# Two transformer blocks in fp32 on one core: eight experts behind branches, or in one pipeline with a late loop

## The chip, the cores and the metric

One Trainium2 chip, one core of it. The metric is the device time of one execution in microseconds, lower is better. The kernel before was timed three times. Its profile is of one further execution.

## The reference

The input is one sequence of 256 tokens with 1024 features, all fp32. A first block of two layers (feed-forward parts, an attention and recurrence mixer, a short convolution mixer) is followed by a second block of two layers. The last sub-layer of the second block is a mixture of experts, and it is where the change lies:

```python
logits = x @ w_router + b_router            # 256 tokens x 8 experts
top_vals, top_idx = top_k(logits, 2)        # softmax over the two gives the weights
y[token] = sum over its two experts e of weight * (silu(x @ w_gate[e]) * (x @ w_up[e])) @ w_down[e]
```

w_gate and w_up are 1024 x 3584 for each expert, w_down is 3584 x 1024. After it come a gate row, a scaled residual and a layer norm. With 256 tokens and two experts each there are 512 places, 64 for an expert on average.

## The kernel before

**Tiles.** Every weight matrix is read in units: unit n is 1 MB of gate and up columns (`w_gu[n]`, 128 hidden columns of each) and 0.5 MB of down rows (`w_d[n]`). The mixture has 8 x 28 = 224 units. SyncE issues the loads (`load_moe_gu` L338, `load_moe_d` L346) into four buffers each, and a load waits until VectorE is through with the unit that lay there, four units earlier. Each fp32 weight is split in two fp32r parts: ScalarE makes the high part (`moe_hi_gu` L622, `moe_hi_d` L629), VectorE the low part (`moe_lo_gu` L1285, `moe_lo_d` L1290). The split parts have two buffers each. A product is three matmuls, high by high, high by low, low by high (`mm3`, L1565 to L1567).

**A mixture step.** For unit i TensorE does gate and up (`slot_gate_up`, 24 matmuls over 256 columns), transposes the product h of unit i - 1 (L1964) and adds the down product of unit i - 2 (`slot_down`, 6 matmuls over 512 columns) to PA. ScalarE does silu (L654), the high part of h (L660), the high parts of units i + 2 (gate and up) and i (down). VectorE does the product with up (L1302), the low part of h (L1308), and the low parts of units i - 1 (down) and i + 2 (gate and up).

**Slots.** The tokens of an expert are gathered into 128 slots by a one-hot matmul (L1917). The outcome of an expert is copied from PA to YS by ScalarE (L689), multiplied by the transposed one-hots with the weights (`scatter_previous`, L1924) at steps 3 and 5 of the following expert, and added to ACC by VectorE (L1314). The next tokens are gathered at steps 16 and 17.

**Branches.** The router's result is counted per expert (`members`, s5i). Before the first expert ScalarE, VectorE and TensorE each load all eight counts into registers (L702, L1407, L2057). Each expert then stands in an If on its count: `sparse(e)` for up to 128 tokens (L1345, L671, L1976), `dense(e)` over all 256 tokens otherwise (L1376, L691, L2032). The bodies of all experts are written out one after the other, with short loops (`Fori`) inside. `sparse(e)` ends with its own pipeline empty: the last two down products and the copy to YS are inside it.

```python
                    with pe.If(counts[e] <= P):
                        sparse(e)
                    with pe.Else():
                        dense(e)
```

**In front of the mixture.** `pre(b)` transposes the normalized tokens (L1621), ScalarE and VectorE scale them into XTF (`modulated`, L449 and L845) and split XTF into XH and XL (`high` L460, `low` L852). TensorE waits for all of XL (L1896) and then computes the logits (L1899) from XTF. VectorE makes the residual (L869, L872), clears ACC (L1229), and does the routing in small operations (L1232 to L1262).

**Behind it.** TensorE scatters the last expert (L1924 into acc), VectorE applies the gate row and the layer norm (L905 to L919), ScalarE its squares and roots (L410, L393, L400), SyncE writes the two halves out.

Of the kernel before, what the change touches and what calls it, by code (L numbers as in the profile page):

```python
# [22 lines left out]
F32 = mybir.dt.float32  # L23
F32R = mybir.dt.float32r
I32 = mybir.dt.int32
ALU = mybir.AluOpType
# [3 lines left out]
P = 128  # L30
# [69 lines left out]
def program(nc, A, out):  # L100
    with ExitStack() as ctx:
# [48 lines left out]
        def view(at, n):  # L150
# [71 lines left out]
        members = s5i[0:1, 0:NE]  # L222
# [41 lines left out]
            "acc", "wT_sb", "hf", "hT", "hh", "gate", "base")}  # L264

# [103 lines left out]
        def _(act):  # L369
# [43 lines left out]
            def pre(b):  # L413
# [52 lines left out]
                for j in (0, 1):  # L466
                    modulated(j)
                high(0)
# [175 lines left out]
            def moe(b):  # L644
# [17 lines left out]
                def sparse_step(i, at, first=False):  # L662

                    silu(i, at, P)
                    if not first:
# [5 lines left out]
                def sparse(e):  # L671
                    at = e * NF2
                    sparse_step(0, at, first=True)
                    for i in range(1, 8):
                        sparse_step(i, at)
                    with act.Fori(0, 2) as j:
                        for i in range(8, 12):
                            sparse_step(i, at + j * 4)
                    for i in range(16, 20):
                        sparse_step(i, at)  # L680
                        if e + 1 < NE and i in (17, 18):
                            gathered(e + 1, i - 17)
                    for i in range(20, NF2):
                        sparse_step(i, at)
                    moe_hi_d(NF2 - 1, at)
                    h_hi(NF2 - 1, at)
                    moe_hi_gu(NF2 + 1, at)
                    act.wait_ge(d_used, at + N0 + NF2)
                    act.activation(YS, tile2(PA[:, 0:2, :]), ACT.Copy).then_inc(moe_s["y"], 1)  # L689

                def dense(e):  # L691
                    with act.Fori(0, NF2 // 4) as j:
                        for i in range(4):
                            at = e * NF2 + j * 4
                            silu(i, at, S)
                            moe_hi_gu(i + 2, at)
                            moe_hi_d(i, at)
                    if e + 1 < NE:
                        gathered(e + 1, 0)
                        gathered(e + 1, 1)  # L700
# [24 lines left out]
        def _(dve):  # L725
# [93 lines left out]
            def pre(b):  # L819
# [36 lines left out]
                if b > SECOND:  # L856
                    dve.wait_ge(xn_done, 2 * b)
                low(0)
# [360 lines left out]
            def moe(b):  # L1219
# [42 lines left out]
                dve.tensor_copy(s5i[:, 0:NE], PB[:, 2, 48:56]).then_inc(moe_s["routed"], 1)  # L1262
# [3 lines left out]
                def onehots(dst, e, weight):  # L1266
                    for t in range(NT):
                        where = place[:, t, e:e + 1]
                        if weight:
                            last = TS(dst[:, t], SLOT, where, share[:, t, e:e + 1], ALU.is_equal, ALU.mult)  # L1270
# [64 lines left out]
                def sparse_step(i, at, first=False, last=False):  # L1335

                    if not last:
                        gated(i, at, P)
                    if not first:
                        h_lo(i - 1, at, PA[:, 2 + (N0 + i - 1) % 2, 0:P], P)  # L1340
                        moe_lo_d(i - 1, at)
                    if not last and i < NF2 - 1:
                        moe_lo_gu(i + 2, at)

                def sparse(e):  # L1345
                    at = e * NF2
                    sparse_step(0, at, first=True)
                    for i in range(1, 9):
# [868 lines left out]
```

## Time and profile before

| | us |
|---|---|
| median of 3 runs | 3064.76 (3061.61 to 3068.96) |
| the profiled execution's own time | 3065.1 |
| span of its profile | 3063.3 |
| outside the span | 1.8 |
| PE, DVE, ACT, POOL busy, share of the span | 87%, 74%, 48%, 31% |
| mixture, first gate-and-up matmul to the last copy to YS | 1933.1 to 3044.3 |

Times in rows are microseconds from the start of the span. Engines are PE (TensorE matmuls), PEld (its weight loads), DVE (VectorE), ACT (ScalarE), POOL (GpSimd), SP (SyncE). A name with a q behind it is the engine's sequencer. The number in square brackets behind a row is the idle time of the engine just before, and what ended it; "issue" means that nothing in the profile was waited for. Matmuls overlap, so their durations are longer than the distance from one to the next. PEclk is the granted TensorE clock, 1.00 for 2.4 GHz and 0.50 for 1.2 GHz.

### The profile page before, as it was taken

How to read it: one execution, taken by the hardware profiler on the slowest of the kernel's cores; microseconds unless marked ns; L12 is line 12 of the kernel's file. 1: busy time of each engine (PE TensorE's matmuls, PEld its weight loads, DVE VectorE, ACT ScalarE, POOL GpSimd, SP SyncE). 2: the span in 40 equal slices, each digit the busy share in tenths (PEclk: the TensorE clock that was granted, in tenths of full speed). 3: DMA queues.
4: the chain of work that ended last, by engine and by line, in shares of the span. 5: the costliest groups of instructions: out<-in, count | busy, mean ns of one | idle time of the engine just before them, and what ended most of it. 6: DMA issues, size and time to landing. Idle time of an engine off the chain costs nothing.

```text
span 3063.3 us, 46911 instructions
## 1 busy us (share of the span) xinstructions
PE 2679.0 (87%) x17674; PEld 2428.0 (79%) x17674; DVE 2255.6 (74%) x2506; ACT 1468.6 (48%) x1892; POOL 953.6 (31%) x568
## 2 busy tenths in 40 slices
PE   8997699999988995569996556899999999999998
PEld 7997589999977984359995435788898989898887
DVE  6676467767768556957677695787787878787788
ACT  4343443433443342043333203676666767676666
POOL 6960079699128003308995330000000000000000
PEclk9998699999999996789997687899999999999999
DMA  7753167577444541137752113698898889798876
GB/s 293 259 192 131 62 228 253 213 253 252 150 161 157 185 156 61 35 110 267 256 199 85 61 35 117 252 341 301 298 343 308 327 299 338 300 343 296 331 278 238
DMA packets 129229, 670.87 MB, mean 219 GB/s; under 512 B 14672, under 2 KB 14992, under 8 KB 80064
## 3 DMA queue, kind: packets, MB, share of 16 engines
q1 hardware_dynamic: 111024, 604.72, 53.7%
q0 software_dynamic: 18064, 64.21, 6.1%
q8 instruction: 96, 1.57, 0.2%
q14 instruction: 45, 0.37, 0.0%
HBM read 667.82 MB, written 1.05 MB: 218 GB/s over the span
## 4 chain that ended last, share of the span: by engine, by line
PE 78%; DVE 14%; ACT 4%; issue 3%; POOL 1%; DMA 1%; ACTq 0%; SPq 0%; DVEq 0%
PE work L1565 16%; PE work L1566 15%; PE work L1567 15%; PE acc L1565 8%; PE acc L1567 8%; PE acc L1566 8%; DVE wl_gu L1285 1%; DVE scratch L1194 1%; ACT wh_gu L622 1%; PE work L1917 1%; PE work L1924 1%; PE acc L1964 1%; DVE wl_gu L735 1%; DVE rows L1133 1%; DVE xT_lo L832 1%
## 5 line engine op out<-in xcount | busy, mean ns | idle before, releaser
L1565 PE MATMUL work<-xT_hi,wh_gu 128*128 128x256 f32 x2120 | 610.7, 288 | 49.9 <-DVE xT_lo L852 19.5
L1566 PE MATMUL work<-xT_lo,wh_gu 128*128 128x256 f32 x2120 | 608.5, 287 | 0.0
L1567 PE MATMUL work<-xT_hi,wl_gu 128*128 128x256 f32 x2120 | 607.4, 287 | 0.0
L1565 PE MATMUL work<-wh_gu,mixT_hi 128*128 128x256 f32 x1792 | 522.7, 292 | 43.2 <-issue 27.8
L1566 PE MATMUL work<-wl_gu,mixT_hi 128*128 128x256 f32 x1792 | 513.2, 286 | 2.6 <-issue 2.6
L1567 PE MATMUL work<-wh_gu,mixT_lo 128*128 128x256 f32 x1792 | 512.5, 286 | 0.2 <-issue 0.2
L735 DVE TENSOR_TENSOR wl_gu<-raw_gu,wh_gu 128x2048 fp32r<-128x2048 f32 x158 | 390.5, 2471 | 124.5 <-ACT wh_gu L375 124.0
L1565 PEld LDWEIGHTS work<-xT_hi,wh_gu 128*128 128x128 f32 x2120 | 415.3, 196 | 60.3 <-issue 35.2
L1566 PEld LDWEIGHTS work<-xT_lo,wh_gu 128*128 128x128 f32 x2120 | 415.9, 196 | 4.8
L1567 PEld LDWEIGHTS work<-xT_hi,wl_gu 128*128 128x128 f32 x2120 | 415.2, 196 | 0.0
L1565 PEld LDWEIGHTS work<-wh_gu,mixT_hi 128*128 128x128 f32 x1792 | 348.9, 195 | 59.2 <-issue 37.6
L1565 PE MATMUL acc<-wh_d,h_hi 128*128 128x512 f32 x912 | 379.3, 416 | 10.2 <-DVE wl_d L1290 8.5
L740 DVE TENSOR_TENSOR wl_d<-raw_d,wh_d 128x1024 fp32r<-128x1024 f32 x157 | 244.7, 1559 | 169.5 <-ACT wh_d L382 169.5
L1566 PEld LDWEIGHTS work<-wl_gu,mixT_hi 128*128 128x128 f32 x1792 | 349.8, 195 | 13.5 <-issue 6.1
L1566 PE MATMUL acc<-wl_d,h_hi 128*128 128x512 f32 x912 | 359.9, 395 | 0.0
L1567 PE MATMUL acc<-wh_d,h_lo 128*128 128x512 f32 x912 | 359.7, 394 | 0.0
L375 ACT ACTIVATE wh_gu<-raw_gu 128x2048 fp32r<-128x2048 f32 x158 | 301.3, 1907 | 112.6 <-PE acc L1567 62.8
L1567 PEld LDWEIGHTS work<-wh_gu,mixT_lo 128*128 128x128 f32 x1792 | 349.1, 195 | 0.6 <-issue 0.5
L382 ACT ACTIVATE wh_d<-raw_d 128x1024 fp32r<-128x1024 f32 x157 | 166.4, 1060 | 294.8 <-PE acc L1567 287.1
L1498 POOL TENSOR_TENSOR scratch<-scratch 128x1024 f32<-128x1024 f32 x84 | 292.2, 3478 | 7.0
L1285 DVE TENSOR_TENSOR wl_gu<-raw_gu,wh_gu 128x2048 fp32r<-128x2048 f32 x113 | 259.1, 2293 | 36.9 <-ACT wh_gu L622 36.7
L1285 DVE TENSOR_TENSOR wl_gu<-scratch,wh_gu 128x2048 fp32r<-128x2048 f32 x112 | 256.6, 2291 | 38.2 <-ACT wh_gu L622 37.9
(436 smaller groups left out, 4899.0 us busy)
## 6 DMA issues: line engine op xcount, KB each, us to landing
raw_gu<-in_w_gu SPq DMA_DIRECT2D x271, 1024.0 KB, 4.9
raw_d<-in_w_d SPq DMA_DIRECT2D x269, 512.0 KB, 5.1
scratch<-in_w_gu SPq DMA_DIRECT2D x112, 1024.0 KB, 7.0
scratch<-in_w_d SPq DMA_DIRECT2D x112, 512.0 KB, 7.7
scratch<-in_w_mod POOLq DMA_DIRECT2D x96, 512.0 KB, 3.7
scratch<-in_s_b POOLq DMA_DIRECT2D x16, 256.0 KB, 3.0
rows<-in_norm_post POOLq DMA_DIRECT2D x6, 512.0 KB, 4.3
rows<-in_ln_g POOLq DMA_DIRECT2D x4, 512.0 KB, 4.4
```

Source lines behind the costliest of these rows:

```text
L375: act.activation(wh_gu[k][:, :, :, :].rearrange("p a k n -> p (a k n)"), raw_gu[k][:, :], ACT.Copy).then_inc(gu_hi, 1)
L382: act.activation(wh_d[k][:, :], raw_d[k][:, :], ACT.Copy).then_inc(d_hi, 1)
L622: act.activation(wh_gu[n % 2][:, :, :, :].rearrange("p a k n -> p (a k n)"), RAW_GU[k] if k > 1 else RAW_GU[k][:, :], ACT.Copy).then_inc(g ...
L735: TT(wl, raw_gu[k][:, :], wh.bitcast(F32), ALU.subtract).then_inc(gu_lo, 1)
L740: TT(wl_d[k][:, :], raw_d[k][:, :], wh_d[k][:, :].bitcast(F32), ALU.subtract).then_inc(d_lo, 1)
L832: last = STT(XL[:, k, tok], turned(t, k), C("norm_pre", 8 * b + k), XH[:, k, tok].bitcast(F32), ALU.mult, ALU.subtract)
L1133: TT(SC[:, 0:2], SC[:, 0:2], MT.rearrange("p (w h i) -> p w h i", w=2, h=4), ALU.add).then_inc(g["masked"], 1)
L1285: TT(wl, RAW_GU[k] if k > 1 else RAW_GU[k][:, :], wh.bitcast(F32), ALU.subtract).then_inc(gu_lo, 1)
L1498: TT(acc, acc, MW[n % 3], ALU.add).then_inc(mod_term, 1)
L1565: pe.matmul(out_, w[0], m[0], start=start, stop=False)
L1566: pe.matmul(out_, w[0], m[1], start=False, stop=False)
L1567: return pe.matmul(out_, w[1], m[0], start=False, stop=stop)
```

## The change

The eight Ifs and all of `dense` go. The steps of all experts form one pipeline: step 0 of an expert also does the transpose of the previous expert's unit 27 and the down product of its unit 26, and step 1 the down product of its unit 27. ScalarE's copy to YS moves into step 1 of the next expert. Only the last expert drains. The one-hots of an expert are made by VectorE just ahead of its step 0. ScalarE and VectorE each have one more loop over steps 20 to 27. In the last expert, ScalarE and VectorE now do the high and low part of the unit behind the last one (`moe_hi_gu(29)`, `moe_lo_gu(29)`) inside step 27, ahead of the last down unit. The counts are replaced by the largest of them (`most_members`), one register load for each engine behind the last expert, and an If around a loop for tokens beyond 128 slots. In `pre`, the split of XTF is left out for the mixture, and TensorE waits for XTF alone.

```diff
+        most_members = s5i[0:1, NE:NE + 1]
         # pre(b), ScalarE (VectorE has modulated(3), modulated(5))
+                if b == len(SUBS) - 1:
+                    modulated(2)
+                    modulated(4)
+                    return
         # ScalarE, moe
-                    if i < NF2 - 1:
-                        moe_hi_gu(i + 2, at)
-                        moe_hi_d(i, at)
+                    moe_hi_gu(i + 2, at)
+                    if i == 1 and e:
+                        act.wait_ge(d_used, N0 + at)
+                        act.activation(YS, tile2(PA[:, 0:2, :]), ACT.Copy).then_inc(moe_s["y"], 1)
+                    moe_hi_d(i, at)
...
-                counts = [act.value_load(members[:, e:e + 1], min_val=0, max_val=S) for e in range(NE)]
-                for e in range(NE):
-                    with act.If(counts[e] <= P):
-                        sparse(e)
-                    with act.Else():
-                        dense(e)
+                h_hi(NF2 - 1, (NE - 1) * NF2)
+                act.wait_ge(d_used, N0 + NE * NF2)
+                act.activation(YS, tile2(PA[:, 0:2, :]), ACT.Copy).then_inc(moe_s["y"], 1)
+
+                most = act.value_load(most_members, min_val=0, max_val=S)
+                with act.If(most > P):
...
         # VectorE, moe
-                dve.tensor_copy(s5i[:, 0:NE], PB[:, 2, 48:56]).then_inc(moe_s["routed"], 1)
+                link(dve.reduce_max(w1[:, 0:1], PB[:, 2, 48:56], AX.X))
+                dve.tensor_copy(s5i[:, NE:NE + 1], w1[:, 0:1]).then_inc(moe_s["routed"], 1)
+                def step(i, at, e=0):
+
+                    gated(i, at, P)
+                    if i or e:
+                        h_lo(i - 1, at, PA[:, 2 + (N0 + i - 1) % 2, 0:P], P)
+                        moe_lo_d(i - 1, at)
+                    moe_lo_gu(i + 2, at)
+
+                for e in range(NE):
+                    at = e * NF2
+                    last = onehots(WGT, e, True)
+                    if e + 1 < NE:
+                        last = onehots(ONE, e + 1, False)
+                    last.then_inc(moe_s["onehots"], 1)
+                    for i in range(8):
+                        step(i, at, e)
...
+                at = (NE - 1) * NF2
+                h_lo(NF2 - 1, at, PA[:, 2 + (N0 + NF2 - 1) % 2, 0:P], P)
+                moe_lo_d(NF2 - 1, at)
+
+                most = dve.value_load(most_members, min_val=0, max_val=S)
+                with dve.If(most > P):
...
         # TensorE, moe
-                pe.wait_ge(xt_l, 4 * (b + 1))
+                pe.wait_ge(xt_f, 4 * (b - SECOND + 1))
+                pe.wait_ge(xt_raw, 2 * (b - SECOND + 1))
...
+                    pe.wait_ge(moe_s["xg_l"], 2 * e + 2)
                     slot_gate_up(0, at, xg)
+                    if e:
+                        h_transpose(-1, at)
+                        slot_down(-2, at, False, False)
                     slot_gate_up(1, at, xg)
                     h_transpose(0, at)
+                    if e:
+                        slot_down(-1, at, False, True)
                     slot_gate_up(2, at, xg)
                     h_transpose(1, at)
                     if e:
                         pe.wait_ge(moe_s["y"], e)
                     slot_down(0, at, True, False)
...
+                h_transpose(NF2 - 1, at)
+                slot_down(NF2 - 2, at, False, False)
+                slot_down(NF2 - 1, at, False, True)
+
+                most = pe.value_load(most_members, min_val=0, max_val=S)
+                with pe.If(most > P):
+                    pe.wait_ge(moe_s["y"], NE)
+                    with pe.Fori(0, NE) as e:
...
```

The lines beginning with # in this diff are headings. The late body is, for each of the 8 experts, one gather (16 matmuls), two transposes, a loop over the 28 units with its own loads on ScalarE's queue and single buffers (24 matmuls, a transpose, 6 matmuls, each step waiting for the one before), and one scatter (4 matmuls).

## Rows read from the trace of the kernel before

**Rows 1.** Page, the chain that ended last, by engine.

```profile
PE 78%; DVE 14%; ACT 4%; issue 3%; POOL 1%; DMA 1%; ACTq 0%; SPq 0%; DVEq 0%
```

**Rows 2.** Busy by window: us, PE, PEld, DVE, ACT, POOL, PEclk, DMA share, GB/s.

```profile
2120.00:2150.00 30.00, 30.00 (x215) 28.14 (x214) 26.84 (x29) 21.78 (x29) 0.00 (x0) 1.00 0.97 360
...
2069.10:2073.90 4.80, 4.80 (x22) 4.80 (x23) 0.00 (x0) 0.00 (x0) 0.00 (x0) 0.50 0.62 254
2074.80:2077.70 2.90, 2.90 (x25) 2.90 (x26) 0.82 (x2) 2.64 (x3) 0.00 (x0) 1.00 0.02 6
```

**Rows 3.** Timeline, ACT silu: steps 2 and 27 of experts 0, 1, 7.

```profile
1946.44 0.28 ACT L654 ACTIVATE scratch<-work 128x128 f32<-128x128 f32 x1 [2.91 <-PE work L1567]
2059.42 0.28 ACT L654 ACTIVATE scratch<-work 128x128 f32<-128x128 f32 x1 [1.18 <-PE work L1567]
...
2082.69 0.28 ACT L654 ACTIVATE scratch<-work 128x128 f32<-128x128 f32 x1 [1.53 <-PE work L1567]
...
2199.10 0.28 ACT L654 ACTIVATE scratch<-work 128x128 f32<-128x128 f32 x1 [1.18 <-PE work L1567]
...
2920.12 0.28 ACT L654 ACTIVATE scratch<-work 128x128 f32<-128x128 f32 x1 [0.65 <-PE work L1567]
...
3038.27 0.28 ACT L654 ACTIVATE scratch<-work 128x128 f32<-128x128 f32 x1 [1.18 <-PE work L1567]
```

**Rows 4.** Waits, 1942 to 3041 us: total us, times, longest us.

```profile
PE work L1565 <- issue: 27.8, 7, 4.8
...
PE work L1565 <- DVE wl_gu L1285: 12.2, 8, 2.7
```

**Rows 5.** Branches of the experts on TensorE (2000:3043) and VectorE: ns min/median/max.

```profile
L2060 PEldq COMPARE_BRANCH  x15: 78/3807/6207, 2063.7 to 3042.6; - x15
...
L1413 DVEq COMPARE_BRANCH  x16: 43/47/54, 1937.6 to 3042.9; - x16
```

**Rows 6.** Timeline, one steady step of expert 1.

```profile
2123.56 2.29 DVE L1285 TENSOR_TENSOR wl_gu<-raw_gu,wh_gu 128x2048 fp32r<-128x2048 f32 x1 [0.35 <-ACT wh_gu L622]
...
2125.64 0.28 ACT L654 ACTIVATE scratch<-work 128x128 f32<-128x128 f32 x1 [1.17 <-PE work L1567]
...
2126.95 0.28 PE L1565 MATMUL work<-wh_gu,mixT_hi 128*128 128x256 f32 x1
```

**Rows 7.** Down weights: timeline of issue and use, then issue to landing.

```profile
2119.05 1.06 ACT L629 ACTIVATE wh_d<-raw_d 128x1024 fp32r<-128x1024 f32 x1
...
2122.18 0.51 SPq L346 DMA_DIRECT2D raw_d<-in_w_d  x1
...
2132.15 1.05 ACT L629 ACTIVATE wh_d<-raw_d 128x1024 fp32r<-128x1024 f32 x1
...
DMA to landing us min/median/max: 5.4/7.8/9.7
```

**Rows 8.** Timeline, in front of the mixture and its first steps.

```profile
1904.09 1.18 ACT L460 ACTIVATE xT_hi<-scratch 128x512 fp32r<-128x512 f32 x2
...
1906.32 0.79 ACT L449 ACTIVATE scratch<-acc,cols 128x128 f32<-128x128 f32 x2
...
1908.91 6.97 PE L1899 MATMUL work<-router_w,scratch 128*128 128x8 f32 x32 [5.48 <-DVE xT_lo L852]
...
1936.14 1.28 ACT L654 ACT_TABLE_LOAD   x1 [3.96 <-issue]
...
1937.46 0.61 DVE L1270 TENSOR_SCALAR scratch<-scratch,small 128x128 f32<-128x128 f32 x2 [4.56 <-issue]
...
1941.89 0.58 PE L1565 MATMUL work<-wh_gu,mixT_hi 128*128 128x256 f32 x1 [2.69 <-DVE wl_gu L1285]
```

**Rows 9.** Timeline, the end of the last expert.

```profile
3042.88 2.29 DVE L1285 TENSOR_TENSOR wl_gu<-raw_gu,wh_gu 128x2048 fp32r<-128x2048 f32 x1 [0.38 <-ACT wh_gu L622]
...
3044.26 1.02 ACT L689 ACTIVATE scratch<-acc 128x1024 f32<-128x1024 f32 x1 [1.41 <-PE acc L1567]
...
3046.55 5.37 PE L1924 MATMUL acc<-scratch 128*128 128x512 f32 x8 [2.32 <-issue]
```

More of the change, by code:

```diff
@@ L264, in program @@
             "acc", "wT_sb", "hf", "hT", "hh", "gate", "base")}
+        late = {n: sem("late_" + n) for n in ("gu_landed", "d_landed", "sum", "scattered", "added")}
+        U1, H1 = N0 + NE * NF2, M0 + NE * NF2
         T_OF = {"ab": 16, "mix2": 9}
@@ L702, in moe @@
[L702 to L707 removed]
+                    with act.Fori(0, 2) as j:
+                        for i in range(20, 24):
+                            step(i, at + j * 4)
+                h_hi(NF2 - 1, (NE - 1) * NF2)
+                act.wait_ge(d_used, N0 + NE * NF2)
@@ L1407, in moe @@
-                counts = [dve.value_load(members[:, e:e + 1], min_val=0, max_val=S) for e in range(NE)]
-                for e in range(NE):
-                    last = onehots(WGT, e, True)
-                    if e + 1 < NE:
-                        last = onehots(ONE, e + 1, False)
-                    last.then_inc(moe_s["onehots"], 1)
-                    with dve.If(counts[e] <= P):
-                        sparse(e)
-                    with dve.Else():
-                        dense(e)
+                            for i in range(8, 12):
+                                step(i, at + j * 4)
@@ new lines, in moe @@
+                        for i in range(16, 20):
+                            step(i, at)
+                            if i in (18, 19):
+                                xg_lo(e + 1, i - 18)
+                        with dve.Fori(0, 2) as j:
+                            for i in range(20, 24):
+                                step(i, at + j * 4)
+                        continue
+                    for i in range(8, NF2):
+                        step(i, at)
+                        if i == 11:
+                            gate_row()
+                        if i in (13, 15, 17, 19):
+                            base((i - 13) // 4, (i - 13) // 2 % 2)
@@ L1974, in slot_down, with step @@
                     last.then_inc(d_used, 1)
-                def sparse(e):
+                pe.wait_ge(moe_s["onehots"], 1)
+                gather(0)
+                gather(1)
+                for e in range(NE):
                     at, xg = e * NF2, e % 2
-                    def step(i, at):
+                    def step(i, at, xg=xg):
                         slot_gate_up(i, at, xg)
@@ L2054, in moe @@
-                pe.wait_ge(moe_s["onehots"], 1)
-                gather(0)
-                gather(1)
-                counts = [pe.value_load(members[:, e:e + 1], min_val=0, max_val=S) for e in range(NE)]
-                for e in range(NE):
-                    pe.wait_ge(moe_s["xg_l"], 2 * e + 2)
-                    with pe.If(counts[e] <= P):
-                        sparse(e)
-                    with pe.Else():
-                        dense(e)
+                h_transpose(NF2 - 1, at)
+                slot_down(NF2 - 2, at, False, False)
```

241 lines of the change are left out of this document (113 added, 128 removed).

## The prediction

> **What bounds the kernel now.** I read the chain of waits on the page first: TensorE carries 78% of it [rows 1]. Then the windows inside the mixture: in 30 us in the middle of an expert TensorE is busy for all 30, at the full clock of 1.00 (2.4 GHz), VectorE for 26.8 and ScalarE for 21.8; the transfers run at 360 GB/s with a share of 0.97 [rows 2]. So a steady step is bound by TensorE, with the transfers close behind. Its length is 4.37 us: the down split on ScalarE starts at 2119.05 and, three steps later, at 2132.15, so 13.10 / 3 [rows 7].
>
> Then the seams between experts, from the times of silu on ScalarE, which follows TensorE's gate and up directly [rows 3]. From silu of step 2 to silu of step 27 take 112.98 us in expert 0, 116.41 in expert 1 and 118.15 in expert 7. Experts 2 to 6 also take 116.41 each. The extra over 25 steps (109.2) is scatter, transposes and gather on TensorE, in expert 7 a wait for the gate row, and all of that stays. From step 2 of expert 0 to step 27 of expert 7 there are 3038.27 - 1946.44 = 1091.8 us; take away 112.98 + 6 x 116.41 + 118.15 = 929.6 and 162.2 us are left for seven seams, 23.2 each. A seam holds three steps, 13.1 us. So a seam loses 10.1 us.
>
> The waits say of what: 27.8 us in seven pieces of "issue", and 12.2 us for the low part of gate and up, of which 2.7 lie in front of the first expert's step 2 and the rest at the seams [rows 4]. The issue time is TensorE's sequencer in its branch at L2060, which takes 3.8 us in the median and up to 6.2, while the branch of VectorE at L1413 takes 0.05 [rows 5]. Behind that idle time TensorE restarts at clock 0.50 (1.2 GHz): 22 matmuls in 4.80 us, 0.218 each, against 25 in 2.90 us, 0.116 each, some microseconds later [rows 2]. 27.8 + 9.5 us are 5.3 us for a seam; the low clock on the 24 to 25 matmuls of step 0 is some 2.5; what is left of the 10.1 is the drain, where the last two down products wait for their splits one after the other.
>
> **The change part by part.** The sum is made against the profiled execution: 3065.1 us, of which the span is 3063.3 and 1.8 lie around it. The median of the runs is 3064.76, so the two are the same for this purpose.
>
> *Seams.* In the new order the matmuls of a seam are the same, and each wait becomes that of a steady step: down product of unit 26 in step 0, of unit 27 in step 1. So a seam costs three plain steps: -7 x 10.08 = -70.5 us. What could be late in its place:
> (a) The copy to YS, 1.02 us [rows 9], now stands on ScalarE in step 1 between two splits. ScalarE idles 1.17 us in each step before silu [rows 6], so it fits, barely. TensorE needs YS free only at the down product of step 2, and behind the copy the down split of unit 1 comes 1 us later, which VectorE takes up only in step 2. Cost 0; without that idle time, up to 1.0 for each seam.
> (b) The one-hots on VectorE, two operations of two instructions, 0.61 us for the first pair [rows 8] and as a bound the same for the second, now stand ahead of step 0. VectorE waits 0.35 us in each step for the high part [rows 6]. Its low part then ends at 2123.56 + 2.29 = 2125.85, and TensorE takes it at 2126.95, so there is another 1.1 us of cover [rows 6]. 1.2 us at most against 1.45: cost 0, at worst 1.2 for each seam.
> (c) The transfers lose the seam's rest. Behind SyncE's issue of a down load at 2122.18 ScalarE uses that slot's unit at 2132.15, 10.0 us later; landing takes 7.8 us in the median, 9.7 at most [rows 7]. A load that lands later than that is covered by ScalarE's 1.17 us. A full expert will take 116.4 + 13.1 = 129.5 us for 28 x 1.573 MB = 44.0 MB, 340 GB/s, under the 360 that the steady window already moves [rows 2]. Cost 0; as an upper bound 1 us for each expert.
>
> The Trainium skill, "DMA: Bandwidth & Descriptors" (Specifications), speaks against this change: it gives some 358 GB/s of HBM for a core. By it a steady step would be bound by memory and take an estimated 1.573 MB / 358 = 4.39 us in place of 4.37, some +5 us over 8 x 25 such steps. This trace is already a little over it, with 360 GB/s at a share of 0.97 [rows 2]; the mechanism is rival 2.
>
> *In front of the mixture.* The logits start at 1908.91. Of their input the last piece on ScalarE is made from 1906.32 to 1907.11, behind three copies into XH of which two take 1.18 us together [rows 8] and the third, of half the width, by an estimate from that row 0.3. Without them the input is complete at about 1905.7, -3.0 us with the waits around it (bounds: -1.8, if ScalarE's piece stays at 1907.1; -6.4, if the logits, 6.97 us for 32 records or 0.218 each, also ran at the full clock's 0.116 [rows 2, 8]). VectorE's residual and clearing of ACC start as much earlier and stay beside the logits. The added maximum over the counts is one small operation in VectorE's chain, +0.2 us.
>
> *First expert.* ScalarE stands 3.96 us and VectorE 4.56 us in "issue", their eight register loads; ScalarE then loads its table for 1.28 us before silu of step 0 [rows 8]. Without the register loads the table load falls in the wait for the first gate and up, and silu, both splits and step 2 of TensorE come 1.3 us earlier: its wait of 2.69 us [rows 8] becomes 1.4. Step 2 also ran at the low clock: silu came 1946.44 - 1941.89 = 4.55 us after its start [rows 3, 8], where 24 matmuls at 0.12 take 2.9. At the seams a wait of some 1.4 us (9.5 / 7, [rows 4]) follows 25 matmuls at the full clock; I take it that the shorter wait here keeps the clock too: -1.65. Together -3.0; bounds -1.0 and -4.5.
>
> *End.* In step 27 of the last expert the split of the unit behind the end is now ahead of the last down split. VectorE's low part of it, 2.29 us, stood behind before, at 3042.88 [rows 9]; in front, it starts when ScalarE has the high part, some 0.6 us after VectorE would have begun with unit 27. I take +1.65 us for the last down product. Before, the scatter then waited for the branch until 3046.55, though the copy to YS was done at 3044.26 + 1.02 = 3045.28 [rows 9], 1.25 us earlier. Now one register load (3.96 / 8 = 0.5 us) and one branch over the late body stand there. Branches over short bodies are those of VectorE, 0.05 us; over the long dense body of TensorE, 3.8 [rows 5]. The late body on TensorE has some 60 matmuls where `dense` has about 280, so I take it as short: the copy sets the start, +1.65 - 1.25 = +0.4. As an upper bound it costs the full 3.8 again: +1.65 + 0.5 = +2.2.
> The Trainium skill, "Runtime: NRT & Kernel Launch" (Instruction fetch mechanics), says that a taken branch whose target isn't in the current two pages has to fetch it first; by it, too, the short body is the cheap case, and the long ones are what the change removes. No row shows the page size.
>
> Sum: -70.5 - 3.0 + 0.2 - 3.0 + 0.4 = -75.9, and 3065.1 - 75.9 = 2989.2. The span would be 2987.4.
>
> **The rivals.**
> 1. *The seam keeps a wait.* (a) and (b) are late together, 1.0 + 1.2 us for each of seven seams, with what (c) adds up to 2989 + 4 to 2989 + 22, so 2993 to 3011, middle 3000. For it: the cover is only 1.17 and 1.45 us for 1.02 and 1.2. Against: the costs fall in different steps on different engines, and a late step is made up in those that follow. Chance 0.13.
> 2. *The transfers fall behind over a full expert*, because the 360 GB/s of 30 us can't be held without the seam's rest. Landing then moves from its median towards its maximum and beyond, by 9.7 - 7.8 = 1.9 us [rows 7], of which ScalarE's idle time hides 1.17 [rows 6]: 0.7 us for each of eight experts, +6, so 2995. The page's rule on the HBM is of this kind. Against: 340 GB/s are wanted on average. Chance 0.08.
> 3. *Only the branch goes.* TensorE still starts an expert with the wait for its low part and the drain's waits, because a split of the next expert is late; only the 27.8 us of issue, the low clock (2.5 us for each seam) and the 6 us in front go: 3065.1 - 27.8 - 17.5 - 6 = 3014. For it: the drain's waits look like VectorE's. Against: in the new order no unit's split depends on the drain. Chance 0.05.
> 4. *The transfers become the bound.* If the average over an expert before (44.0 MB in 116.4 + 23.2 = 139.6 us, 315 GB/s) were what memory gives over a long stretch, the mixture would stay as long as it is, and only the 6 us in front would come: 3059. Against: 360 GB/s over 30 us [rows 2]. Chance 0.03.
> 5. *Slower: the late body is run.* It decides at 129 tokens in the busiest expert, where one If opens the loop for all eight experts. A unit there waits in series for its load (5.4 us at the least [rows 7]), a low part of 2.29 [rows 6], some 2.9 us of gate and up and, as an estimate from these, 2 for a high part and 1 for down: 13 us for 224 units, +2900 us, about 5900. Against: every one of the 8 experts took the slot form before, as its 28 silus of 128 columns show [rows 3]. Chance 0.01.
> 6. *It doesn't do what it says*, because the loops' exits on TensorE, now at the end of each expert, cost what the If cost: nothing gained at the seams, 3060. Against: such exits stand in the middle of the 116.41 us already, without a trace in them. Chance 0.02.
>
> **How the numbers follow.** The forecast itself, 2981 to 2995, has 0.68. The predicted time is that of its middle, 2989. The range takes in its bounds (-3.4 for a full clock under the logits and -1.5 in the first expert below, +1.8 at the end and +2.0 in the first expert above) rival 2 and half of rival 1: 2981 to 3004. A measurement of this kernel tells 0.2%, 6 us, from no change. Faster by more than that: 0.68 + 0.13 + 0.08 + 0.05 = 0.94, and 0.02 of rivals 4 and 6, which lie at the edge: 0.96. Within: 0.03. Slower: 0.01.
>
> **What would show it.** Right: silu to silu across a seam in three steps of 4.37 us, TensorE without "issue" waits in the mixture, granted clock 1.00 from the first expert's step 2 to the last drain, an expert in 129.5 us, no landing that ScalarE waits for, logits 3 us earlier, and the last unit's low part behind that of the unit after it. Wrong: waits of TensorE for a low part in steps 0 to 3, ScalarE's down split waiting for a load, a long branch in front of the last scatter, or any instruction of the late body.

## The result and the profile after

The kernel after takes 2988.94 us (median of four, 2986.70 to 2992.49), beside 3066.86 for the kernel before on the same chip: ratio 0.9747, 95% interval 0.9728 to 0.9767. A second set of five executions, run as the last experiment, gave 2991.48 and 0.9771 (0.9754 to 0.9788). The forecast was 2989.0, 2981 to 3004. The profiled execution took 2992.49 us with a span of 2990.7. One of the six executions of the last version below (both ends put right) ran in a slower state, 3441 us at a granted clock of 0.72, and is left out of its figures.

The chain that ended last, by engine (before: [rows 1]), and two windows, the second over a seam (columns as in [rows 2]):

```profile
PE 80%; DVE 13%; ACT 3%; issue 2%; POOL 1%; DMA 1%; SPq 0%; DVEq 0%; ACTq 0%
```

```profile
2120.00:2150.00 30.00, 30.00 (x222) 28.41 (x221) 23.69 (x25) 21.63 (x31) 0.00 (x0) 1.00 0.94 354
2060.00:2070.00 10.00, 10.00 (x72) 9.34 (x71) 9.63 (x16) 8.03 (x12) 0.00 (x0) 1.00 0.97 373
```

A seam is now full on TensorE at the full clock, as the middle of an expert is. All waits of TensorE from 1942 to 2970 us (before: [rows 4], 27.8 of issue and 12.2 for the low part of gate and up):

```profile
PE work L1647 <- DVE scratch L1343: 3.3, 1, 3.3
PE acc L1580 <- DVE wl_d L1315: 0.4, 1, 0.4
```

The timeline of the first seam, silu of step 27, VectorE's one-hots and its low part behind step 0, the copy to YS, silu of step 2 (before: [rows 3]):

```profile
2056.18 0.28 ACT L661 ACTIVATE scratch<-work 128x128 f32<-128x128 f32 x1 [1.17 <-PE work L1582]
...
2060.67 0.60 DVE L1295 TENSOR_SCALAR scratch<-scratch,small 128x128 f32<-128x128 f32 x2
2061.18 0.48 DVE L1297 TENSOR_SCALAR scratch<-scratch,small 128x128 f32<-128x128 f32 x2
...
2063.10 2.29 DVE L1310 TENSOR_TENSOR wl_gu<-scratch,wh_gu 128x2048 fp32r<-128x2048 f32 x1
...
2067.05 1.02 ACT L677 ACTIVATE scratch<-acc 128x1024 f32<-128x1024 f32 x1
...
2069.28 0.28 ACT L661 ACTIVATE scratch<-work 128x128 f32<-128x128 f32 x1 [0.25 <-PE work L1582]
```

2069.28 - 2056.18 = 13.10 us, and all seven seams take that. Before they took 162.24 together, now 91.70: -70.5. The low part of gate and up starts at 2063.10. The one before it started at 2058.46, and one plain step later would be 2058.46 + 4.37 = 2062.83, so it is 0.27 us late. ScalarE's idle time before silu fell from 1.17 to 0.25. TensorE waits for neither.

In front of the mixture and at its end (before: [rows 8, 9]): logits, first scatter; VectorE's last low parts, TensorE's last down products with their waits.

```profile
1907.82 6.24 PE L1915 MATMUL work<-router_w,scratch 128*128 128x8 f32 x32 [2.40 <-ACT scratch L452]
...
2968.27 2.29 DVE L1310 TENSOR_TENSOR wl_gu<-raw_gu,wh_gu 128x2048 fp32r<-128x2048 f32 x1 [0.35 <-ACT wh_gu L629]
...
2970.68 1.22 DVE L1315 TENSOR_TENSOR wl_d<-scratch,wh_d 128x1024 fp32r<-128x1024 f32 x1
...
2971.95 0.50 PE L1580 MATMUL acc<-wh_d,h_hi 128*128 128x512 f32 x1 [2.32 <-DVE wl_d L1315]
...
2974.73 3.70 PE L1940 MATMUL acc<-scratch 128*128 128x512 f32 x8 [1.11 <-ACT scratch L696]
```

Between landmarks of the two profiled executions (times at which the same instruction starts or ends in both) the 72.6 us between the spans are: seams -70.5; from the end of the second normalization to silu of the first expert's step 2, -5.3 (45.1 to 39.8); from the last silu to the end of the span, -0.3 (25.0 to 24.7); +1.5 inside the last expert (below); and +2.1 in code in front, which is the same in both. That last term is what one execution differs from the next by: the last operation of that normalization starts between 1895.8 and 1902.6 us in the fourteen profiles of before, after and the runs below, and in the two profiles of the kernel after it starts 2.9 us apart (1902.6 and 1899.7).

### The profile page after: what moved, and what is told of

The parts are those of the page before. It is cut to its first block, busy times and chain, and to the rows that moved or that the text cites. A ratio compares the mean times of both kernels' runs of the same rounds, so it can differ in the third digit from the quotient of the medians.

```text
span 2990.7 us, 47279 instructions
## 1 busy us (share of the span) xinstructions
PE 2657.8 (89%) x17674; PEld 2415.1 (81%) x17674; DVE 2255.8 (75%) x2501; ACT 1467.8 (49%) x1886; POOL 954.0 (32%) x568
## 3 DMA queue, kind: packets, MB, share of 16 engines
HBM read 667.82 MB, written 1.05 MB: 224 GB/s over the span
## 4 chain that ended last, share of the span: by engine, by line
PE 80%; DVE 13%; ACT 3%; issue 2%; POOL 1%; DMA 1%; SPq 0%; DVEq 0%; ACTq 0%
PE work L1580 16%; PE work L1581 16%; PE work L1582 16%; PE acc L1580 9%; PE acc L1582 9%; PE acc L1581 9%; DVE scratch L1217 1%; PE work L1933 1%; PE acc L1980 1%; PE work L1940 1%; DVE wl_gu L754 1%; DVE xT_lo L871 1%; DVE rows L1156 1%; DVE xT_lo L851 1%; PE work L1889 1%
## 5 line engine op out<-in xcount | busy, mean ns | idle before, releaser
L1580 PE MATMUL work<-wh_gu,mixT_hi 128*128 128x256 f32 x1792 | 514.3, 287 | 4.5 <-DVE mixT_lo L1303 3.3
L1581 PE MATMUL work<-wl_gu,mixT_hi 128*128 128x256 f32 x1792 | 506.9, 283 | 0.0
L1580 PEld LDWEIGHTS work<-wh_gu,mixT_hi 128*128 128x128 f32 x1792 | 342.3, 191 | 16.8 <-DVE mixT_lo L1303 3.5
L1581 PEld LDWEIGHTS work<-wl_gu,mixT_hi 128*128 128x128 f32 x1792 | 342.8, 191 | 11.6 <-issue 3.3
L1582 PEld LDWEIGHTS work<-wh_gu,mixT_lo 128*128 128x128 f32 x1792 | 342.6, 191 | 0.0
```

Of the source, the lines that this page charges most:

```text
L1580: pe.matmul(out_, w[0], m[0], start=start, stop=False)
L1581: pe.matmul(out_, w[0], m[1], start=False, stop=False)
L1582: return pe.matmul(out_, w[1], m[0], start=False, stop=stop)
```

## The experiments

Where a ratio is given, a run was timed four to six times beside the kernel before. The others are one execution each, with its profile; their totals settle nothing below some 6 us, and what they show is read from their traces.

**What the branch cost, and what the drain.** Two kernels, both the kernel before with its drained pipeline. In the first no expert has an If:

```diff
-    counts = [pe.value_load(members[:, e:e + 1], ...) for e in range(NE)]   # on all three engines
-    with pe.If(counts[e] <= P):
-        sparse(e)
-    with pe.Else():
-        dense(e)
+    sparse(e)
```

> The kernel before with the eight Ifs, the dense bodies and the register loads taken out; sparse(e) stays as it is, with its drain at each expert's end. Theory (a seam's 10.1 us are some 4.3 of branch, 2.5 of low clock behind it and 3.3 of drain and refill): no issue wait of TensorE at the seams, full clock there, a seam of 16.4 us from silu of step 27 to silu of step 2 in place of 23.2, and 3 us less in front of the first expert's step 2: about 3016 us. Rival A (the drain costs nothing by itself, the branch is all): seams of 13.1, about 2992. Rival B (the drain's waits alone are enough to lower the clock): seams of 19, about 3034.

In the second everything stays but most of TensorE's code that is never entered: of some 280 matmuls 14 are left, with the two scatters, which the expectation's 6 doesn't count (the part for more than 128 tokens is left out there).

```diff
     # TensorE, dense(e)
-    with pe.Fori(0, NF2 // 2 - 1) as j: ...
-    for i in (NF2 - 2, NF2 - 1): ...
-    next_tokens(e, 0)
-    next_tokens(e, 1)
```

> The kernel before with Ifs and register loads kept; only the body of dense(e) on TensorE, which is never entered here, is cut from some 280 matmuls to 6. Theory (what costs is how far the taken branch jumps): TensorE's branch at the end of sparse(e) takes under 0.5 us in place of 3.8 to 6.2, seams of 16.4 to 17 us, in all about 3018 us. Rival (an If's exit on TensorE costs this whatever it jumps over, because its queue of matmuls has to be refilled): seams of 23.2 as before, 3066 us.

Measured: 3014.89 us, ratio 0.9832 (0.9817 to 0.9846), and 3016.62, 0.9841 (0.9827 to 0.9855). A seam takes 16.5 us in both, in place of 23.2. The second kernel still has every If and register load; its branch, by the line that was L2060:

```profile
L2050 PEldq COMPARE_BRANCH  x16: 67/126/319, 1929.2 to 2992.4; - x16
```

and TensorE's waits in the mixture, the same in both kernels:

```profile
PE work L1565 <- DVE wl_gu L1285: 10.5, 7, 1.5
PE acc L1565 <- DVE wl_d L1290: 8.4, 16, 0.6
```

So 6.7 us of each seam hung on code of TensorE that is never run. Before, a seam had 4.4 us of issue time: the 27.8 us of [rows 4] and 2.8 more, of which 2.6 lie in the last seam, where TensorE stood still a second time, between two matmuls: 30.6 / 7. The other 2.3 are put down to the low clock behind it, which is a difference and not a row.

```profile
PE work L1566 <- issue: 2.6, 1, 2.6
```

The drain costs the other 3.4 (16.5 - 13.1). The wait for wl_gu, 1.5 us a seam, stands here without any issue time: it is the drain's, not the branch's. With 8.4 / 8 = 1.05 for wl_d these waits are 2.6 of the 3.4; no row names the rest.

The eight register loads are in the second kernel alone. From the first gate and up to silu of step 2 it takes 12.19 us, the first 10.81, but this isn't their price: both wait 1.50 us for wl_gu ahead of step 2, and the 1.4 us lie in step 0, which the second ran at a granted clock of 0.50 in its first 2 us, the first at 1.00. What they cost shows in the kernel before, which ran step 0 at 1.00 too: it waits 2.69 us in place of 1.50, and step 2, at the low clock behind that wait, takes 4.55 us to silu in place of 3.18. Together 2.6 us.

**Half of the code.** Between 280 matmuls (4.4 us of issue time) and 14 (nothing) lies a third length:

```diff
     # TensorE, dense(e) of the kernel before
-    with pe.Fori(0, NF2 // 2 - 1) as j: ...
```

> The kernel before, with the loop over 26 units taken out of the branch for more than 128 tokens on TensorE, which is not entered: the code that is jumped over shrinks from about 280 matmuls to about 160 for each expert; with nearly all of it gone (the run with a short else) the branch took 0.13 us and a seam 16.5. Theory (a far jump costs the same however far): branch of 3.8 us in the median, seam 23.2, total 3065. Rival 1 (the cost grows with what is jumped over): 57% of it, branch 2.2, seam about 20, total 3042. Rival 2 (it is short enough now): seam 16.5, total 3016.

Measured: 3045.80 us, and none of the three. The seven seams take 18.7, 16.5, 22.5, 22.9, 16.5, 23.5 and 24.0 us. The first matmuls behind the five that are not 16.5:

```profile
2067.18 0.28 PE L1565 MATMUL work<-wh_gu,mixT_hi 128*128 128x256 f32 x1 [2.08 <-issue]
...
2335.20 0.38 PE L1565 MATMUL work<-wh_gu,mixT_hi 128*128 128x256 f32 x1 [4.21 <-issue]
...
2474.12 0.37 PE L1566 MATMUL work<-wl_gu,mixT_hi 128*128 128x256 f32 x1 [4.15 <-issue]
...
2746.48 0.57 PE L1565 MATMUL work<-wh_gu,mixT_hi 128*128 128x256 f32 x1 [4.40 <-issue]
...
2887.21 0.57 PE L1565 MATMUL work<-wh_gu,mixT_hi 128*128 128x256 f32 x1 [5.23 <-issue]
```

The branches, and for comparison those of the kernel before:

```profile
L2055 PEldq COMPARE_BRANCH  x16: 67/186/6681, 1931.6 to 3025.3; - x16
```

```profile
L2060 PEldq COMPARE_BRANCH  x16: 78/1948/6207, 1932.9 to 3042.6; - x16
```

Half of the sixteen are the branches into an expert, under 0.1 us each in the kernel before. Of its eight jumps over the unentered body every one is long, 3.8 to 6.2 us. Here three of eight are (5.7, 5.9 and 6.7), and two stalls, of 2.08 and 4.15 us, stand behind jumps of 0.30 and 0.32 us; the second of them comes only after the first matmul of the step. So equal code over an equal distance costs nothing at two seams and at the end, and 2 to 5 us of idle time at five: the length alone doesn't decide. The copies differ in where they lie, and that this decides is the likely reading; no run moved a copy, and whether the same seams are hit in every execution wasn't looked at. The Trainium skill, "Runtime: NRT & Kernel Launch" (Instruction fetch mechanics), has a rule of this kind: a jump out of the two pages at hand waits for a fetch. Over equal code, branches of 5.7 to 6.7 us beside others of 0.3 agree with that; no run shows a page size or the fetch itself. The rows also show the clock: behind 2.08 us of idle time the matmuls go on at 0.28 us (granted clock 1.00 in the next 2.9 us), behind 4.15 us and more at 0.37 to 0.57 (granted clock 0.50 to 0.57).

**The split in front of the logits, put back** into the kernel after:

```diff
     # pre(b), ScalarE and VectorE
-                if b == len(SUBS) - 1:
-                    modulated(2)
-                    modulated(4)
-                    return
     # TensorE
-                pe.wait_ge(xt_f, 4 * (b - SECOND + 1))
-                pe.wait_ge(xt_raw, 2 * (b - SECOND + 1))
+                pe.wait_ge(xt_l, 4 * (b + 1))
```

> The changed kernel with the split of XTF and TensorE's wait for it put back in front of the logits. Theory: the logits start 3.0 to 3.2 us later behind the second normalization, 2992 us. Rival (VectorE's residual and the clearing of ACC bound this stretch anyway): less than 1 us, 2989 to 2990.

Measured: 2995.30 us, ratio 0.9773 (0.9759 to 0.9787), span 2993.2. The logits:

```profile
1909.41 6.96 PE L1906 MATMUL work<-router_w,scratch 128*128 128x8 f32 x32 [5.49 <-DVE xT_lo L867]
```

The wait is 5.49 us again, against 2.40 without the split: 3.1 us. In total the run doesn't settle so small a term; its interval overlaps with the second set of the kernel after. The landmarks do: from the end of the normalization to the start of the logits it is 7.6 us in all profiles with the split and 4.4 in all without it.

**How much cover the seam has on VectorE.** Expectation (b) of the forecast, loaded with more work:

```diff
     # VectorE, ahead of step 0
+    if e:
+        for m in range(4):
+            TS(view(3328 + P * m, P), SLOT, place[...], share[...], ALU.is_equal, ALU.mult)
+        TT(JUNK, X[:, 0, :], X[:, 1, :], ALU.mult)      # the second run alone
     last = onehots(WGT, e, True)
```

> The kernel after, with four more one-hot instructions (128 columns each) ahead of step 0 of experts 1 to 7. The four that are there take VectorE 0.90 us (2060.67 to 2061.57), so these add about as much. In the kernel after, the low part of gate and up in step 0 starts 0.27 us later than in a steady step, and TensorE takes it 1.10 us after its end. Theory (the cover is this 1.10 us): 0.27 + 0.90 = 1.17 late, so a seam from silu of step 27 to silu of step 2 takes 13.1 to 13.2 us, total within 1 us of the kernel after, 2989 us. Rival (each us on VectorE at a seam costs its us): seam 14.0, +6.3 us in all, 2995.

> As the run before, with one VectorE product of 1024 columns more (1.2 us), 2.1 us more than the kernel after at each seam. Theory (cover of 1.10 us, of which 0.27 are used): 0.27 + 2.1 - 1.10 = 1.3 us lost once at each seam, seam 14.4 us, a wait of TensorE for wl_gu in step 2, total 2989 + 9 = 2998; some more if the clock falls behind the wait. Rival (later steps take it up, nothing lost): 2989. Rival (all of it costs): seam 15.2, 3004.

Measured: 2995.91 and 3002.51 us; six seams of 13.48 and of 14.60, and a last one of 13.10 and 14.21. VectorE's low part of step 0 in the one and in the other:

```profile
2063.62 2.28 DVE L1310 TENSOR_TENSOR wl_gu<-scratch,wh_gu 128x2048 fp32r<-128x2048 f32 x1
```

```profile
2065.47 2.28 DVE L1310 TENSOR_TENSOR wl_gu<-scratch,wh_gu 128x2048 fp32r<-128x2048 f32 x1
```

By their own step 27 (2057.95 and 2058.66, plus 4.37) they are 1.30 and 2.44 us late, and the seams lose 0.38 and 1.50: both give a cover of 0.93 us. It is a threshold, beyond which each microsecond costs one, for each expert. The last seam fits it: the last expert has no next one and two one-hot instructions less, some 0.4 us, so the low part is 0.9 and 2.05 us late, within the cover in the one run and 1.1 beyond it in the other. I had taken 1.10, the time from the end of the low part to the matmul. But TensorE waits for the low part ahead of the step's first weight load, though that load takes the tokens and not the low part, and it starts 0.23 us before the first matmul. In the kernel after, step 2 behind the first seam:

```profile
2065.98 0.19 PEld L1580 LDWEIGHTS work<-wh_gu,mixT_hi 128*128 128x128 f32 x1
...
2066.21 0.28 PE L1580 MATMUL work<-wh_gu,mixT_hi 128*128 128x256 f32 x1
```

The kernel after is 0.27 late, so 0.66 us are left. The first run's seam lies between its theory (13.1 to 13.2) and its rival (14.0). That its total is the rival's 2995 is chance: the seams give 2.3 us, and 1.3 are a low clock in the last expert, of the kind told below.

**How much cover there is on ScalarE.**

```diff
     # ScalarE, step 1
     act.wait_ge(d_used, N0 + at)
+    act.activation(JUNK, tile2(PA[:, 0:2, :]), ACT.Copy)
     act.activation(YS, tile2(PA[:, 0:2, :]), ACT.Copy).then_inc(moe_s["y"], 1)
```

> The kernel after, with the copy to YS preceded by a second copy of the same 1024 columns to a place that nobody reads, 1.02 us more on ScalarE in step 1 of experts 1 to 7. ScalarE's idle time of 1.17 us in a step then falls short by 0.87. Theory (a late high part meets the same 1.10 us ahead of TensorE, and the next step's idle time takes up the rest): seam 13.1 us, total 2989. Rival (what does not fit in ScalarE's idle time is lost): seam 14.0, total 2995.

Measured: 2991.64 us. Silu of step 2 comes 0.52 us later (seam 13.62), and silu of step 27 comes 115.88 us behind it in place of 116.40: an expert takes 129.50 us as before. A second microsecond on ScalarE costs nothing over an expert: silu comes late once and has caught up by step 27.

**The transfers: one buffer fewer, and less work on TensorE.**

```diff
     # SyncE, load_moe_gu and load_moe_d
-    ge(sp, gu_lo, n - 3, dyn)
+    ge(sp, gu_lo, n - 2, dyn)
...
-    ge(sp, d_lo, n - 3, dyn)
+    ge(sp, d_lo, n - 2, dyn)
```

> The kernel after, with every load of the mixture issued one unit later (SyncE waits for VectorE to be through with the unit three earlier, not four; three buffers in effect). Issue to use falls from 10.0 to some 5.6 us, against a landing of 5.4 us at the least and 7.8 in the median. Theory (the four buffers carry the transfers, and their slack of 1 to 6 us is real but no more than a step): ScalarE waits for landings in nearly all steps, steps of 5 to 6.5 us, total 3100 to 3400. Rival (landing gets as short as the least once fewer loads are under way, so that the order alone decides): steps of 4.4 us, under 3000.

```diff
     # TensorE, slot_gate_up
-    last = mm3(PB[...], (XGH[xg][:, k, :], XGL[xg][:, k, :]), (wh_gu..., wl_gu...), ...)
+    pe.matmul(PB[...], XGH[xg][:, k, :], wh_gu[n % 2][:, :, k, :], ...)
+    last = pe.matmul(PB[...], XGH[xg][:, k, :], wl_gu[n % 2][:, :, k, :], ...)
```

> The kernel after, which leaves out the product of the high part of gate and up with the low part of the tokens in the mixture: 16 matmuls of 0.12 us in a step in place of 24, TensorE then needs 3.41 us in a step of 4.37. Theory (the transfers are the next bound, at the 360 GB/s and share of 0.97 of the steady window, so 371 GB/s at a share of 1): plain steps of 4.24 us, some 205 of them, total 2989 - 27 = 2962, DMA share 1.0. Rival 1 (the transfers have room, VectorE with 26.8 us in 30 is next): steps of 3.9, total 2893. Rival 2, a ceiling below the present rate: no gain, 2989. The Trainium skill, page DMA: Bandwidth & Descriptors (Specifications), gives some 358 GB/s of HBM for a core; by it a step would take an estimated 4.39 us.

Measured: 3029.52 us with the later loads. From step 2 of the first expert to step 27 of the last they take 1060.6 us in place of 1022.8: 0.17 us a step. ScalarE's waits in the mixture:

```profile
ACT wh_d L636 <- DMA scratch<-in_w_d: 129.5, 89, 3.4
ACT wh_d L636 <- DMA raw_d<-in_w_d: 129.4, 96, 3.5
```

The kernel after has no such wait. Here they come in 185 of 224 steps, 1.4 us each, and ScalarE's idle time of 1.17 us takes most of it. So the four buffers are needed, but I overrated the price (3100 to 3400) by leaving out that cover, on which I had counted elsewhere. The rival falls too: with fewer loads under way a down load still lands 7.8 us after its issue in the median.

The kernel with two products, which leaves out a third of gate and up, takes 2861.50 us, 127 less. Over the mixture (columns as before), and VectorE in one step:

```profile
1942.00:2832.00 890.00, 855.56 (x5386) 722.60 (x5387) 865.70 (x951) 743.93 (x959) 0.00 (x0) 1.00 0.98 389
```

```profile
2240.06 2.29 DVE L1310 TENSOR_TENSOR wl_gu<-scratch,wh_gu 128x2048 fp32r<-128x2048 f32 x1
2242.26 0.28 DVE L1327 TENSOR_TENSOR scratch<-scratch,work 128x128 f32<-128x128 f32 x1
2242.46 0.29 DVE L1333 TENSOR_TENSOR h_lo<-acc,h_hi 128x128 fp32r<-128x128 f32 x1
2242.66 1.22 DVE L1315 TENSOR_TENSOR wl_d<-raw_d,wh_d 128x1024 fp32r<-128x1024 f32 x1
2243.79 2.29 DVE L1310 TENSOR_TENSOR wl_gu<-scratch,wh_gu 128x2048 fp32r<-128x2048 f32 x1
```

My theory falls, and rival 1 is the one that holds: VectorE is next, without a gap, at 2243.79 - 2240.06 = 3.73 us a step. I had put it at 3.9, from busy times; what counts is the distance from one start to the next. The transfers moved 389 GB/s over 890 us. In plain steps VectorE takes up 1.573 MB / 3.73 = 422 GB/s, some of it out of the buffers. A DMA share of 0.97 was no ceiling at 371. How far it goes beyond this no run shows, and it may not be far: the share is 0.98 here, and ScalarE waits for landings in 117 steps, 57 us in all, nearly all of which VectorE doesn't feel (it is busy for 866 of 890 us). Nor are the 358 GB/s a ceiling here which the Trainium skill, "DMA: Bandwidth & Descriptors" (Specifications), gives for a core: one core by itself took 9% more over the whole mixture.

**The late body, run.**

```diff
-    with pe.If(most > P):      # on all three engines
+    with pe.If(most > 32):
```

> The kernel after, with the late loop's condition changed from more than 128 to more than 32 tokens in the busiest expert, so that it runs with the same input. No token has a slot beyond 128, so it adds zeros. My estimate: each of 224 units takes 13 us in series (load, high and low part, gate and up, silu, transpose, down), so 2989 + 2912 = 5900 us. Rival (the loads of a unit overlap the products of the one before, since ScalarE issues them behind the down product's signal alone): 8 to 10 us a unit, 4800 to 5200.

Measured: 7381.68 us, so (7381.7 - 2989) / 224 = 19.6 us a unit. One unit, by the timeline of ScalarE and VectorE:

```profile
4003.41 1.91 ACT L717 ACTIVATE wh_gu<-raw_gu 128x2048 fp32r<-128x2048 f32 x1 [6.96 <-DMA raw_gu<-in_w_gu]
...
4007.56 1.22 DVE L1420 TENSOR_TENSOR wl_d<-raw_d,wh_d 128x1024 fp32r<-128x1024 f32 x1
...
4014.35 0.28 ACT L722 ACTIVATE scratch<-work 128x128 f32<-128x128 f32 x1 [8.09 <-PE work L1582]
...
4017.88 0.34 ACTq L714 DMA_DIRECT2D raw_gu<-in_w_gu  x1
...
4022.66 1.91 ACT L717 ACTIVATE wh_gu<-raw_gu 128x2048 fp32r<-128x2048 f32 x1 [7.01 <-DMA raw_gu<-in_w_gu]
```

It is all in series, as I had said: load 4.8, high part 1.9, low parts 2.3 and 1.2, gate and up 5.5, silu to the split of h 1.7, down 1.7. My 13 us left out the low part of down and the splits of h, and had gate and up at the full clock: with a TensorE that waits most of the time it takes 5.5 us, at a granted clock of 0.51, in place of 2.9. The cliff at 129 tokens in the busiest expert is +4393 us, 2.5 times the time. What the kernel before takes with such an expert wasn't run.

**The end and the gate row, both put right.** Two things the profile after left: the split of the unit that doesn't exist, ahead of the last down split, and the gate row, for which TensorE waits 3.3 us in the last expert's step 8.

```diff
     # ScalarE and VectorE, last expert, step 27: unit 29's parts behind the last down unit
-    with act.Fori(0, 2) as j: ...
+    for i in range(20, NF2 - 1):
+        step(i, at)
+    silu(NF2 - 1, at, P); h_hi(NF2 - 2, at); moe_hi_d(NF2 - 1, at)
+    h_hi(NF2 - 1, (NE - 1) * NF2)
+    moe_hi_gu(NF2 + 1, (NE - 1) * NF2)
     # TensorE: gate row at steps 16, 17 of the last expert too, not ahead of step 8
-                    if e + 1 == NE:
-                        next_tokens(e, 0)
-                        if e + 1 < NE and i in (16, 17):
+                        if i in (16, 17):
                             next_tokens(e, i - 16)
```

> The changed kernel with two moves: the gate row of the last expert at step 16 in place of step 8 (VectorE's part at 17 to 25), and the split of the unit behind the end after the last down split. Theory: TensorE's wait of 3.3 us and the low clock behind it go from step 8 (11.45 us now), 4.8 us in all; the last down product comes 4.3 us behind the last silu in place of 6.0, 1.65 us: about 2982.5 us. Rival (VectorE has no room for the base rows at steps 19 to 25, and the branch holds the last scatter back): 2987 to 2990.

Measured: 2983.45 us (median of five), ratio 0.9731 (0.9718 to 0.9744). The last down product and the last scatter:

```profile
2962.92 0.50 PE L1590 MATMUL acc<-wh_d,h_hi 128*128 128x512 f32 x1 [0.33 <-DVE wl_d L1323]
...
2965.70 3.70 PE L1950 MATMUL acc<-scratch 128*128 128x512 f32 x8 [1.11 <-ACT scratch L704]
```

With silu of step 27 at 2958.63 they come 4.29 and 7.07 us behind it, against 5.96 and 8.74 in the kernel after: -1.67. The last expert's 25 steps take 114.62 us in place of 119.68. Against its interval that of the first set of the kernel after overlaps, so the kernel after was timed again, which is also the test of how much of this was the clock's:

> The kernel after, unchanged, in five rounds, for the comparison with the version that does both end changes (0.9731 of the kernel before, 0.9718 to 0.9744). Theory (its 5.1 us in the last expert and 1.6 us at the end, as its trace shows them, are there in every execution): 0.9750, 2988 us. Rival (most of them comes from where the clock happened to fall in the one profile of the kernel after): 0.9735 or less, 2984.

Measured: 2991.48 us, 0.9771 (0.9754 to 0.9788). That lies above the theory and above the rival: the two sets of the kernel after differ by more (0.9747 and 0.9771) than theory and rival do. The version with both changes is faster than the kernel after, by 5.2 to 6.7 us between the landmarks of its profile and of these two (1.67 at the end, 3.5 or 5.1 in the last expert), and it is the fastest that was run with the whole computation. Step 8 of the last expert in the first and in the second profile of the kernel after:

```profile
2876.53 2.47 PE L1647 MATMUL work<-const,modT 128*128 128x128 f32 x16 [3.28 <-DVE scratch L1343]
2883.02 0.28 ACT L661 ACTIVATE scratch<-work 128x128 f32<-128x128 f32 x1 [8.26 <-PE work L1582]
...
2877.00:2880.50 3.50, 3.50 (x23) 3.50 (x22) 0.00 (x0) 0.00 (x0) 0.00 (x0) 0.64 0.94 317
```

```profile
2873.59 2.05 PE L1647 MATMUL work<-const,modT 128*128 128x128 f32 x16 [3.28 <-DVE scratch L1343]
2878.55 0.28 ACT L661 ACTIVATE scratch<-work 128x128 f32<-128x128 f32 x1 [6.73 <-PE work L1582]
...
2874.00:2877.50 3.50, 3.50 (x32) 3.50 (x31) 0.00 (x0) 0.00 (x0) 0.00 (x0) 1.00 0.82 270
```

Same kernel, same wait of 3.28 us, clock 0.64 once and 1.00 once: 1.5 us. So 1.5 of the 5.1 us were chance, and 3.5 are the wait itself. The kernel before has this wait too; its last expert took 118.15 us, as in the second profile.

## Why the prediction was right, point by point

The seams carry the forecast, and they came as reasoned. That the median meets 2989 to 0.1 us is luck: the two sets of the kernel after differ by 2.5 us, and between the two profiles the change is -72.6, not -75.9, of which +2.1 in front and +1.5 in the last expert are what one execution differs from the next by.

- **Seams**, -70.5: measured -70.5. The step was sound since it set a measured seam against three measured steps, and needn't know what the 10.1 us were made of. That division was partly wrong: the branch had 6.7 (I gave it 5.3 + 2.5, with the wl_gu waits in it), the drain 3.4 (I left it 2.3, and it is wl_gu's wait that belongs to it). I had also misread [rows 5]: 3.8 us isn't the median of the branches that cost, since the row mixes them with the short ones into an expert. It is the shortest of the eight; their median is 5.3.
- **(a) and (b)**, the covers: 0 each, confirmed. In (b) the one-hots take 0.90 us (2060.67 to 2061.57) and the low part is 0.27 late, so VectorE's own idle time took up 0.63 (I had 0.35), and behind it are 0.93 (I had 1.10): 1.56 in all, against my 1.45. (a) has more room than I gave it.
- **(c)**, transfers: no landing was waited for. Landing 7.9 us in the median, 10.1 at most, with 10.0 to go by and ScalarE's idle time behind: the four buffers carry it, three don't.
- **Logits**, -3.0: the wait is 3.1 us shorter (5.48 to 2.40). Their own 6.2 to 7.0 us hang on the clock (see the first expert).
- **First expert**, -3.0: the register loads are gone from the path, and "the shorter wait here keeps the clock too" held: step 2 takes 3.18 us to silu in place of 4.55. But from the start of gate and up to silu of step 2 it was 13.36 us and is 12.07 and 12.04 in the two profiles of the kernel after, -1.3 only. What the sum lacked is the clock of step 0: granted 0.50 from 1933 to 1935 us, before 1.00 there.

```profile
1933.00:1935.00 2.00, 2.00 (x11) 2.00 (x11) 0.00 (x0) 0.00 (x0) 0.00 (x0) 0.50 0.00 0
```

  Where it stays full, as in the improved version with the same code, the stretch takes 10.81: -2.5, with a wait for step 2 of 1.50, where I had 1.4. In the four runs of the seam and of the later loads, again with the same code there, step 0 runs at 0.50 throughout and the stretch takes 13.2. So the code gives -2.5, and the clock takes 0 to 2.4 of it back. The logits make up for part of this: 6.24 us at a partly full clock in the kernel after, 6.97 in the improved version. So logits and first expert together gave -5.3 (the improved version -5.7) for the -5.8 of the sum (-3.0 + 0.2 - 3.0).
- **End**, +0.4: down product 5.96 us behind the last silu, before 4.29, so +1.67 (I had +1.65); the branch over the short late body took 0.37 us, before 3.8; scatter +0.46. The scatter then ran at the full clock, 3.70 us in place of 5.37, which I hadn't counted; to the end of the span the whole is -0.3.
- **Rivals.** 1 and 2 didn't come, and the runs say by how little: 0.66 us on VectorE, one buffer. 3 was priced at 3014; the run with a short else is its seam without the 6 us in front, and took 3016.6, so the whole case would have come to 3011. 4 and the rule of the Trainium skill on the HBM had no ground: 389 GB/s were moved with two products. 5 was the right mechanism at two thirds of its price (13 for 19.6 us a unit). 6 didn't come: TensorE has no issue wait left in the mixture.

## What to carry to other kernels

Price the removal of a seam as measured seam less measured plain steps, and price what moves into its place by the idle time of the engine that takes it, to the engine that needs the outcome, down to the first instruction there that waits for it, which can be a weight load. A branch on TensorE can cost microseconds for code that is never run, and a second time by the clock it restarts at. With half of the code some jumps are free and some aren't, so leave no long body behind a branch on the path that is taken, or keep one branch behind everything. Terms of 1 to 3 us are read between landmarks of the trace, not from totals that differ by 6 us from run to run.

## What was not expected of the hardware

- A busy share of the DMA engines of 0.94 to 0.97 at 354 to 373 GB/s left room: 389 GB/s over 890 us at 0.98.
- Of eight jumps over equal code three cost nothing and five 2.1 to 5.2 us of idle time.
- Behind the same wait of 3.28 us TensorE's clock was 0.64 in one execution and 1.00 in the next, and the first expert's step 0 ran at 0.50, 0.85 or 1.00 with the same code.
